# Dense steps that read their moving tile and write their result from the last column to the first

## The reference, cut to what matters

```python
x = layer_norm(x, ln_in_g, ln_in_b)
proj = x @ w_in                                   # 1024 -> 9 * 256 columns
# four mixers read proj: RG-LRU, short gated conv, stick-breaking attention, causal pooling
out = jnp.concatenate([ya, yb, yc, yd], axis=-1) @ w_out          # 1024 -> 1024
x = layer_norm(ALPHA * x + out, ln1_g, ln1_b)
x = layer_norm(ALPHA * x + jnp.square(jax.nn.relu(x @ w_ff1)) @ w_ff2, ln2_g, ln2_b)   # 1024 -> 4096 -> 1024
```

## Time and profile before

| | |
|---|---|
| median of 3 runs | 2443.58 us (2443.28 to 2446.14) |
| span of the profiled execution | 2440.8 us, 36724 instructions |
| median above that span | 2.8 us |
| TensorE busy | 2406.7 us, 99% of the span |
| VectorE, ScalarE, GpSimd busy | 65%, 53%, 10% |
| mean DMA rate | 144 GB/s |

### The profile page before, as it was taken

How to read it: one execution, slowest core, us unless ns; L and a number is a source line. 1 busy time by engine, 2 the same in 40 slices (tenths; PEclk the granted TensorE clock), 3 DMA queues, 4 the chain that set the end, 5 groups by cost and what they waited for, 6 DMA issues and landing times.

```text
span 2440.8 us, 36724 instructions
## 1 busy us (share of the span) xinstructions
PE 2406.7 (99%) x13263; PEld 2331.5 (96%) x13263; DVE 1585.0 (65%) x2233; ACT 1286.6 (53%) x1982; POOL 243.0 (10%) x527
## 2 busy tenths in 40 slices
PE   7999999999999999999999999999999999999998
PEld 7999999999999999999999999999999999999998
DVE  7635662656777787777788777757655665764335
ACT  5466523555655745656555565554455555444432
POOL 0012320200001100011100111000122130000000
PEclk9999999999999999999999999999999999999999
DMA  8434554534444434444443443333566674343332
GB/s 257 153 108 143 159 174 138 184 111 130 162 134 139 142 110 144 150 129 144 128 124 117 137 141 124 125 122 114 182 187 187 209 234 134 120 136 117 112 118 83
DMA packets 141526, 351.64 MB, mean 144 GB/s; under 512 B 20625, under 2 KB 64146, under 8 KB 141218
## 3 DMA queue, kind: packets, MB, share of 16 engines
q1 hardware_dynamic: 128994, 312.88, 40.6%
q0 software_dynamic: 12352, 36.42, 4.7%
HBM read 300.11 MB, written 49.12 MB: 143 GB/s over the span
## 4 chain that ended last, share of the span: by engine, by line
PE 95%; DVE 2%; ACT 2%; DMA 1%; issue 1%; SPq 0%; DVEq 0%; ACTq 0%
PE PS L1136 22%; PE PS L1138 22%; PE PS L1137 22%; PE PS L874 5%; PE PS L872 5%; PE PS L873 5%; PE PS L942 2%; PE PS L964 1%; PE PS L932 1%; PE PS L963 1%; PE PS L1026 1%; PE PS L933 1%; PE PS L1056 1%; PE PS L1014 1%; PE PS L912 1%
## 5 line engine op out<-in xcount | busy, mean ns | idle before, releaser
L1440 ACT ACTIVATE w_hi_lo<-w_raw 128x1024 fp32r<-128x1024 f32 x240 | 252.7, 1053 | 283.5 <-PE PS L1138 277.3
L1136 PE MATMUL PS<-a_hi,w_hi_lo 128*128 128x416 f32 x1080 | 385.1, 357 | 1.3 <-DVE w_hi_lo L1995 1.3
L1138 PE MATMUL PS<-a_hi,w_hi_lo 128*128 128x416 f32 x1080 | 379.3, 351 | 0.0
L1137 PE MATMUL PS<-a_lo,w_hi_lo 128*128 128x416 f32 x1080 | 378.6, 351 | 0.0
L1995 DVE TENSOR_TENSOR w_hi_lo<-w_raw,w_hi_lo 128x1024 fp32r<-128x1024 f32 x240 | 292.6, 1219 | 58.1 <-ACT w_hi_lo L1440 55.9
L1136 PE MATMUL PS<-h_hi,w_hi_lo 128*128 128x416 f32 x824 | 294.6, 358 | 0.0
L1138 PE MATMUL PS<-h_hi,w_hi_lo 128*128 128x416 f32 x824 | 290.2, 352 | 0.0
L1137 PE MATMUL PS<-h_lo,w_hi_lo 128*128 128x416 f32 x824 | 289.4, 351 | 0.0
L2022 DVE TENSOR_TENSOR h_lo<-h_full,h_hi 128x416 fp32r<-128x416 f32 x160 | 94.6, 592 | 222.9 <-ACT h_hi L1455 222.8
L1136 PEld LDWEIGHTS PS<-a_hi,w_hi_lo 128*128 128x128 f32 x1080 | 203.0, 188 | 4.1 <-DVE w_hi_lo L1995 1.7
L1137 PEld LDWEIGHTS PS<-a_lo,w_hi_lo 128*128 128x128 f32 x1080 | 203.5, 188 | 2.1
(11 more groups left out here) (336 smaller groups left out, 5203.8 us busy)
## 6 DMA issues: line engine op xcount, KB each, us to landing
w_raw<-w_all SPq DMA_DIRECT2D x380, 512.0 KB, 3.5
proj_scratch<-stage SPq DMA_DIRECT2D x70, 208.0 KB, 1.9
k_rows<-kv_out SPq DMA_DIRECT2D x80, 128.0 KB, 4.0
v_hi_lo<-v_scratch SPq DMA_DIRECT2D x40, 256.0 KB, 4.1
x_scratch<-x_full SPq DMA_DIRECT2D x20, 416.0 KB, 2.9
x_residual<-x_scratch SPq DMA_DIRECT2D x5, 1664.0 KB, 7.6
pages<-ck SPq DMA_DIRECT2D x64, 128.0 KB, 2.2
pages<-ck POOLq DMA_DIRECT2D x64, 128.0 KB, 2.5
```

Of the source, the lines that this page charges most:

```text
L1136: pe.matmul(out, w_h, mh_[:, k, :], start=(g == 0), stop=False)
L1137: pe.matmul(out, w_h, ml_[:, k, :], start=False, stop=False)
L1138: ins = pe.matmul(out, w_l, mh_[:, k, :], start=False, stop=(g == KT - 1))
L1440: act.activation(halves(w_hi(n)), raw_halves(n), ACT.Copy).then_inc(s_wh, 1)
```

## The change

In `dense` the three matmuls get their moving operand and their output as views that run from the last column to the first. Column j of the result is still made of column j of the input and lies at the same place; only the order in which the 416 columns are read and written is turned round. The weights are passed as before. `project` and `last_tiles` and all other matmuls stay as they are. No instruction, wait, buffer or DMA is added, moved or removed.

```diff
                     w_h, w_l = w_at(w_hi(n), k), w_at(w_lo(n), k)
-                    pe.matmul(out, w_h, mh_[:, k, :], start=(g == 0), stop=False)
-                    pe.matmul(out, w_h, ml_[:, k, :], start=False, stop=False)
-                    ins = pe.matmul(out, w_l, mh_[:, k, :], start=False, stop=(g == KT - 1))
+                    pe.matmul(rev(out), w_h, rev(mh_[:, k, :]), start=(g == 0), stop=False)
+                    pe.matmul(rev(out), w_h, rev(ml_[:, k, :]), start=False, stop=False)
+                    ins = pe.matmul(rev(out), w_l, rev(mh_[:, k, :]), start=False, stop=(g == KT - 1))
```

## The result

The changed kernel takes 2451.53 us, the median of 5 runs (2450.14 to 2454.71), against 2443.58 us (2442.99 to 2446.14). The ratio is 1.0035 with a 95% interval from 1.0025 to 1.0046. It is 8 us slower, where 28 us less was forecast; the time lies inside the stated range.

What follows compares the result with a forecast made beforehand. The prediction took TensorE, busy 99% of the span, to bound the kernel. Span 2440.8 + 2.8 around it = 2443.6 us, less 28 (8616 dense matmuls x 3.3 ns), gave 2415 us; range 2366 to 2495.

Steps and rivals of the forecast that it cites:

- What bounds the kernel, and by how much a nanosecond counts: TensorE, busy 99%, sets the time; one nanosecond on each of 8616 dense matmuls is 8.6 us.
- The rate of a view with step minus one: Dense matmuls' turned views: taken to run at no cost; upper bound 161 ns each, +1390 us.
- How often the two streams meet: Moving tile and next weights' load in dense matmuls: same direction, fewer meetings, 3.3 ns less each, 28 us.
- The weights of a step stay hidden: Weight preparation on ScalarE (1.05 us) and VectorE (1.22 us) stays covered by the 4.53 us step; gain not eaten up.
- Nothing happens: Dense matmuls: loss is the moving stream's alone, or meetings cost by time spent; 2443 us, chance 0.25.
- A little slower: Dense matmuls: buffer offsets 0, 64, 192 suit the old order, so losses rise; +5 ns, +43 us, chance 0.13.
- Held behind the weights: First 108 ns of dense matmuls: moving stream held to weight load's pace; +100 to +333 us, chance 0.15.
- Half rate: Dense matmuls: turned view read or written at half the rate, about 350 ns each; 3834 us, chance 0.07.

Runs made afterwards that it cites:

- e2_write_only: Against the kernel before, only the result of the dense matmuls written from the last column, the moving operand read forward: 2443.88 us, ratio 1.0003.

## Why the prediction was wrong, point by point

**What bounds the kernel, and by how much a nanosecond counts.** Right. TensorE's pace is the time: +1.12 ns per pair of starts, by some 8180 such pairs, is 9.2 us, and +9.0 was found in the dense lines. (The seven distances at the lower clock are in the trace before and not in the one after; they take 1.1 us off this difference.)

**The rate of a view with step minus one: no cost.** Right, for the write to within the measurement (e2_write_only), for the read to within 0.3 ns of 189.5 on the mean over placings; whether these 0.3 ns are a cost of the direction is open. The row of VectorE's scans pointed the right way, though it was from another engine.

**How often the two streams meet: two thirds of the varying part goes, -28 us.** This is the step that failed, in sign. It rested on two inferences. First, that equal matmuls that take 345 to 355 ns show meetings with the weight load: something of the load is in it, as its placing moves the mean by up to 2.6 ns. (These lengths have modelled ends; the distances between starts spread further, from 182 to 198 ns with a mean of 188.8, and would have been the better row.) Second, that fewer meetings cost less, in proportion to the relative path during the load. The short load refutes that: a quarter of the load leaves the loss at 15.7 ns. What the runs showed in its place: the part of the loss that the change moves depends on how the weights are placed to the moving tile, and its sign with it: turning costs 1.12 ns per matmul as the kernel was, 2.05 at distance 0, and gains 1.4 at 160. At the placing of this kernel 18% of the distances were 185 ns or less; turned round there is one such distance in all the kernels with whole loads. So the spread was read at the wrong end: the shortest duration was not what remains when meetings are gone, but a pace that the matmuls reach in order at good placings, and the change closed it off.

**The weights of a step stay hidden.** Right: the waits of line 1136 are 1.1 and 1.1 us.

**The rivals.** "Nothing happens" is refuted by the interval. "A little slower" was the mechanism at work, at 0.13, for some seven tenths of the loss: the offsets of 0, 64 and 192 bytes suit the streams as they ran. Its size, +5 ns from the longest equal matmul, was over four times too large: the median went up to that longest value, but the median is not the mean. "Held behind the weights" would have shown as a pace of over 200 ns; none of the turned kernels has one above 190.1 on the mean. "Half rate" is out. That the measured time lies inside the range is due to these first two rivals, which the range took in, and not to the mechanism of the forecast: a hit by width.

**The rule on two read ports** ("TensorE: Matmul & The Clock Gate", Step-by-step, in the Trainium skill: a load takes no bandwidth from the running matmul). The short load agrees in bulk: the pace does not rise when the load is cut to a quarter. It does not hold to the last per cent, since moving the weights by 160 bytes, with nothing else changed, takes the mean distance of dense starts from 188.0 to 190.6 ns. The page's N / 2.4 + 2.5 ns would be 175.8 for 416 columns and 89.2 for 208; measured are 188.8 and, with short loads, 95.9. Here the measurement decides.

**What stays open.** Why 0 is good and 160 is bad for columns in order, what the 9 to 16 ns of loss at the upper clock are made of, and whether it is the direction against the load or the place where the stream starts that bars the short distances. Turning moves that start by 1660 bytes, 124 within a line, so it is a new placing as well as a new direction; but the lowest pace in order, 188.1 to 188.6 ns, stands nowhere in the turned row of the table, whose lowest is 189.25, so a shift along the row in steps of 32 bytes does not give the one from the other. The runs show which placing does what, not the machinery.

## What to carry to other kernels

When TensorE sets the time to 99%, a per cent hides in how the addresses of the moving tile and of the weights lie to each other: put the weight buffers at one distance, sweep it in steps of 32 bytes, and read the distance between starts by buffer before trying anything cleverer. Read it by line too: a placing that the whole kernel shares also moves matmuls that the edit does not touch, here the projection, and a kernel's time then mixes the two. An edit of the address order must be judged at more than one placing: here the same three lines gave +15, +8 and -9 us. The version that beats both kernels is columns in order with `W_AT = (0, 0, 0)`, 2437.06 us, 0.26% below the kernel before. And a spread among equal instructions is no proof of what is behind it: cut the suspected cause (here the load, to a quarter) before building a forecast on it.

## What was not expected of the hardware

A 128-column load of float32 weights beside a matmul of 416 columns costs no more than a 32-column load (188.8 against 189.0 ns). Beside 208 columns it does: in the halved steps of `last_tiles` the distance from line 1161 to line 1162 is 111 ns in the kernel before, where short loads gave 95.9. The pace of fp32r matmuls at 2.4 GHz has a part that grows with the columns beyond one per clock (95.9 ns at 208, 189.0 at 416: 0.448 ns a column, where one clock is 0.417), and at 1.2 GHz it has none (346.7 and 173.3 ns, one column per clock). The distances between starts of equal matmuls tend to fall into groups: their counts peak at 184, 187, 190 and 192 ns in the kernel before, and at 183, 187 to 188 and 192 with all weights at distance 0.
